# Inverses of 64x64 triangular blocks: 16x16 diagonal blocks by substitution on VectorE, and the old scan between its parts

## The chip, the cores and the metric

The kernel runs on one core of a Trainium2 chip. The metric is the time of one execution on the device in microseconds (us). TensorE is PE below, VectorE DVE, ScalarE ACT and GpSimd POOL.

## What is computed

A network in fp32 over 256 tokens of width 1024: two layers (feed-forward, three token mixers side by side, cross attention, feed-forward), and then one block with attention, a gated delta rule in both directions and a convolutional feed-forward. Two of the mixers are recurrences that are worked in chunks of 64 tokens, and each needs the inverse of a unit triangular 64x64 matrix per head and chunk. For the gated delta rule the reference says it so:

```python
kk = jnp.einsum('bhncd,bhnsd->bhncs', k, k)
a_mat = jnp.where(strict, beta[..., :, None] * dec * kk, 0.0) + jnp.eye(GDN_CHUNK, dtype=jnp.float32)
rhs = jnp.concatenate([beta[..., None] * v, (beta * jnp.exp(gam))[..., None] * k], axis=-1)
uw = lax.linalg.triangular_solve(a_mat, rhs, left_side=True, lower=True, unit_diagonal=True)
...
def step(s, inp):
    delta = u_c - jnp.einsum('bhcd,bhde->bhce', w_c, s)
    s_new = gl_c[..., None, None] * s + jnp.einsum('bhcd,bhce->bhde', kd_c, delta)
```

The layers' mixer (rwkv) is a recurrence per token in the reference; the kernel works it in chunks too, with an inverse of the same kind.

## The kernel before

`Inverse` inverts 16 tiles of 128x128, each with two 64x64 blocks on its diagonal, in 4 groups of 4 tiles, two groups (a pair) at a time with their instructions alternating. It goes by doubling: at level l (0 to 5) the inverses of blocks of size 2^l are joined to blocks of 2^(l+1). POOL makes the part of the matrix that belongs to the level (`inv_m` = `inv_d` x a mask), PE multiplies it by X, ACT copies the product to `inv_t`, PE multiplies that by the transposed inverse (`xt`) and by itself turned round, and DVE subtracts both results from X and `xt`. X and `xt` hold the inverse and its transpose. Level 0 is the identity minus the masked part (L1247). In the second block there is a seventh step, the join, which goes from 64 to 128.

The users are two. `rwkv_stage`, in each of two layers: 16 masked products `lt` on DVE (L1387), then the inverse, then `attention_stage`, which holds the layer's scan. And `gdn_stages`, with four quarters q (direction d = 0, 0, 1, 1, and half of the heads): per quarter four heads' matrices (`GdnMatrices`, the last product of each is L2717), then the inverse, then in the next quarter its scan (`GdnScan`, 12 steps). Steps 0 to 3 of the scan of q-1 lie between the matrices of q. Steps 4 to 11 are a chain in four rounds: PE multiplies by the state (L2779), DVE makes `gdelta` (L2817) and `gdk` (L2821), PE multiplies (L2786), DVE updates the state (L2830); in the last two rounds PE makes outputs (L2792, L2793), which ACT copies (L2851) for d = 0 and DVE adds (L2837) for d = 1. In the kernel before each of the steps 4 to 11 is issued ahead of one pair's level of the inverse of q, on PE, DVE and ACT alike:

```python
mats[q].inv.pe(pe, between=lambda pair: scan_step(pe, 4 + pair))
```

After quarter 3 the last scan is run alone ("quarter 4"). All engines execute in the order of their own queue and wait on semaphores. `K.dve_own.after` makes DVE wait for its own last instruction.

Of the kernel before, what the change touches and what calls it, by code (L numbers as in the profile page):

```python
# [35 lines left out]
LEVELS = 6  # L36
# [7 lines left out]
class Counted:  # L44


    def __init__(self, sem):
        self.sem = sem
        self.n = 0
# [23 lines left out]
def constant_tables():  # L73
# [23 lines left out]
    parts["blockident"] = brow == bcol  # L97
    for l in range(LEVELS):
# [3 lines left out]
    parts["levels_back"] = np.concatenate([m[1] for m in lev], 1)  # L102
    strict, incl = same & (row < col), same & (row <= col)
# [1070 lines left out]
class InversePlaces:  # L1174


    def __init__(self, K, ctx, groups, own_xt):
        f = lambda name: [K.sb(f"{name}{i}", [P, 4, CH], ctx=ctx) for i in range(2)]
        self.X, self.T1 = f("inv_x"), f("inv_t")
        self.diag = [K.sb(f"inv_d{g}", [P, 4, CH], ctx=ctx) for g in range(groups)]  # L1180
        self.xt = f("inv_xt") if own_xt else None
        self.mask = [[K.sb(f"inv_m{s}{j}", [P, 4, CH], ctx=ctx) for j in range(2)] for s in range(2)]


class Inverse:


    BLOCK_LEVELS = 6
    PER_GROUP = property(lambda self: self.BLOCK_LEVELS + (self.join is not None))

    def __init__(self, K, places, tag, groups, masks, lt, before, xt=None, join=None, bank=4):
        self.K, self.groups, self.masks = K, groups, masks
        self.lt, self.before, self.join = lt, before, join
# [4 lines left out]
        self.X, self.T1, self.diag, self.mask = places.X, places.T1, places.diag, places.mask  # L1198
        self.xt = xt or (lambda g: places.xt[g % 2][:, :, :])
# [4 lines left out]
        self.steps = [(pair * 2 + s, l) for pair in range(groups // 2) for l in range(self.PER_GROUP) for s in range(2)]  # L1204
        self.index = {st: i for i, st in enumerate(self.steps)}
        self.update = {st: i for i, st in enumerate([st for st in self.steps if st[1] > 0])}
        self.masked = {st: i for i, st in enumerate([st for st in self.steps if st[1] < self.BLOCK_LEVELS])}

    def finished(self, eng):

        eng.wait_ge(self.uv_ready, len(self.update))
        eng.wait_ge(self.t_copied, len(self.steps))
        eng.wait_ge(self.x_ready, len(self.update))
        if self.join is not None:
            eng.wait_ge(self.kept, 2 * self.groups)

    def final(self, g):

        return self.update[(g, self.PER_GROUP - 1)] + 1

    PAIRS = property(lambda self: len(self.steps) // 2)
    HALVES = (slice(0, CH), slice(CH, P))
# [5 lines left out]
    def pool(self, pool):  # L1228
        K = self.K
        for g, l in self.masked:  # L1230
            s = g % 2
            m = self.mask[s][l % 2]
            if l == 0:
                pool.wait_ge(self.d_ready, 2 * g + 2)
            if l >= 2:
                pool.wait_ge(self.t_ready, self.index[(g, l - 2)] + 1)
            elif g >= 2:
                pool.wait_ge(self.t_ready, self.index[(g - 2, self.BLOCK_LEVELS - 2 + l)] + 1)
            level = K.c(self.masks, first=l * CH, n=CH).unsqueeze(1).to_broadcast([P, 4, CH])
            ins = pool.tensor_tensor(m[:, :, :], self.diag[g][:, :, :], level, ALU.mult)  # L1240
            if l == 0:
                K.pool_own.after(pool, ins)
                if self.join is not None and g >= 2:
                    pool.wait_ge(self.x_ready, self.final(g - 2))
                    pool.wait_ge(self.kept, 2 * (g - 2) + 2)
                ident = K.c("blockident").unsqueeze(1).to_broadcast([P, 4, CH])
                ins = pool.tensor_tensor(self.xt(g), ident, m[:, :, :], ALU.subtract)  # L1247
            ins.then_inc(self.m_ready, 1)

    def blocks(self, pe, bank, lhsT, rhs):  # L1250

        for q in range(4):
            for half in self.HALVES:
                last = pe.matmul(bank[half, q * CH:(q + 1) * CH], lhsT[half, q, :], rhs(half, q), start=True, stop=True)  # L1254
        return last

    def pe(self, pe, between=lambda pair: None):

        K = self.K
        for i0 in range(0, len(self.steps), 2):  # L1260
            between(i0 // 2)
            for i in (i0, i0 + 1):
# [3 lines left out]
                X = lambda half, q: self.X[s][half, q, :]  # L1266
                if l == 0:
                    pe.wait_ge(self.m_ready, self.masked[(g, 0)] + 1)
                    last = self.blocks(pe, bank, self.xt(g), lambda half, q: K.c("blockident", half))
                elif l < self.BLOCK_LEVELS:  # L1270
                    pe.wait_ge(self.m_ready, self.masked[(g, l)] + 1)
                    if l == 1:
                        pe.wait_ge(self.t_copied, self.index[(g, 0)] + 1)
                    else:
                        pe.wait_ge(self.x_ready, self.update[(g, l - 1)] + 1)
                    last = self.blocks(pe, bank, self.mask[s][l % 2], X)
                else:
                    src, dst = self.joined()
                    pe.wait_ge(self.x_ready, self.update[(g, l - 1)] + 1)
                    for q in range(4):  # L1280
                        last = pe.matmul(bank[dst, q * CH:(q + 1) * CH], self.lt(g)[src, q, dst], X(src, q),
                                         start=True, stop=True)
                last.then_inc(self.t_ready, 1)
            if self.steps[i0][1] == 0:
                continue
            for i in (i0, i0 + 1):
# [3 lines left out]
                if l == 1 and g >= 2:  # L1290
                    pe.wait_ge(self.x_ready, self.final(g - 2))
                xt = lambda half, q: self.xt(g)[half, q, :]
                if l < self.BLOCK_LEVELS:
                    if l < self.PER_GROUP - 1:
                        self.blocks(pe, self.first_bank(s), self.xt(g), lambda half, q: self.T1[s][half, q, :])
                    last = self.blocks(pe, self.second_bank(s), self.T1[s], xt)
                else:
                    src, dst = self.joined()
                    for q in range(4):
                        last = pe.matmul(self.second_bank(s)[src, q * CH:(q + 1) * CH], self.T1[s][dst, q, :],  # L1300
                                         xt(dst, q), start=True, stop=True)
# [12 lines left out]
    def act(self, act, between=lambda pair: None, first=0):  # L1314
        for g in range(first, 2):
            self.diagonal(act, g)
        for i, (g, l) in enumerate(self.steps):
# [3 lines left out]
            if l == 2 and g + 2 < self.groups:  # L1321
                self.diagonal(act, g + 2)
            act.wait_ge(self.t_ready, i + 1)
            dst = self.X[s] if l == 0 else self.T1[s]
            rows = slice(0, P) if l < self.BLOCK_LEVELS else self.joined()[1]
            act.copy(dst[rows, :, :], self.psum(self.first_bank(s), rows)).then_inc(self.t_copied, 1)  # L1326
            if l == self.BLOCK_LEVELS:
                act.wait_ge(self.x_ready, self.update[(g, l - 1)] + 1)
# [3 lines left out]
    def dve(self, dve, between=lambda pair: None):  # L1332
        for i, (g, l) in enumerate(self.steps):
            if i % 2 == 0:
                between(i // 2)
            if l == 0:
                continue
            s = g % 2
            dve.wait_ge(self.uv_ready, self.update[(g, l)] + 1)
            if l < self.BLOCK_LEVELS:  # L1340
# [1907 lines left out]
```

## Time and profile before

| | us |
|---|---|
| median of 3 runs | 2956.34 (2944.53 to 2960.41) |
| the profiled execution | 2961.04 |
| its span | 2959.2 |
| PE busy | 2557.3 |
| DVE busy | 1139.4 |
| ACT busy | 1144.0 |
| POOL busy | 1303.1 |

The span is what the profile covers of the profiled execution. The granted clock is TensorE's as a share of its full 2.4 GHz (0.50 is 1.2 GHz); its mean over the execution is 0.912. In rows of the timeline the columns are start, duration, engine, line, operation, output<-inputs, shapes, count, and in brackets the engine's idle time ahead of it with what ended that.

### The profile page before, as it was taken

What the parts mean: (1) busy time and instruction counts of PE and PEld (TensorE: products, weight loads), DVE (VectorE), ACT (ScalarE), POOL (GpSimd) and SP (SyncE); (2) the same over time, 40 slices, a digit from 0 to 9 for tenths busy, and PEclk for the clock granted to TensorE, in tenths of its full rate; (3) what the DMA queues carried; (4) which work ended last, traced back from release to release, by engine and by line L of the source; (5) the groups of instructions that cost most, each with busy time, mean ns of one, the idle gap of its engine ahead of it and who ended that gap; (6) DMA issues with size and microseconds to landing.
All of it is one profiled execution on the core that took longest, in us unless ns stands there. A gap on an engine that the chain in (4) does not pass through costs nothing. (4 is left out here: it accounts for less than half of the span.)

```text
span 2959.2 us, 50697 instructions
## 1 busy us (share of the span) xinstructions
PE 2557.3 (86%) x22003; PEld 2228.7 (75%) x22003; DVE 1139.4 (39%) x2055; ACT 1144.0 (39%) x1567; POOL 1303.1 (44%) x452
## 2 busy tenths in 40 slices
PE   5998988886998998988977899699889997787878
PEld 4997865385997998966466899567667776787878
DVE  2113654332111111754242211276636664334990
ACT  4433422334443433422334442447833331533333
POOL 2774520151775774610043586322222121674655
PEclk8999988987999999988986999899979998898998
DMA  4554401431554554500432354422000000553432
GB/s 148 181 172 132 129 2 43 142 125 47 170 167 137 170 173 122 171 15 16 128 114 86 114 185 129 130 72 68 19 2 2 2 2 3 184 169 110 144 127 93
DMA packets 298722, 306.64 MB, mean 104 GB/s; under 512 B 7249, under 2 KB 294461, under 8 KB 298493
## 3 DMA queue, kind: packets, MB, share of 16 engines
q1 hardware_dynamic: 298493, 303.32, 31.9%
q8 instruction: 176, 2.88, 0.4%
q14 instruction: 53, 0.43, 0.0%
HBM read 302.25 MB, written 1.05 MB: 102 GB/s over the span
## 5 line engine op out<-in xcount | busy, mean ns | idle before, releaser
L360 POOL TENSOR_TENSOR slab_lo<-ring,slab_hi 128x2048 fp32r<-128x2048 f32 (+1 forms) x242 | 1096.2, 4539 | 1044.4 <-ACT slab_hi L351 1044.3
L351 ACT CAST slab_hi<-ring 128x2048 fp32r<-128x2048 f32 (+1 forms) x242 | 450.8, 1867 | 639.4 <-PE bank L383 579.2
L381 PE MATMUL bank<-ffn_h_hi,slab_hi 128*128 128x256 f32 x1408 | 402.5, 286 | 23.1 <-DVE ffn_h_lo L423 23.1
L382 PE MATMUL bank<-ffn_h_lo,slab_hi 128*128 128x256 f32 x1408 | 401.7, 285 | 0.0
L383 PE MATMUL bank<-ffn_h_hi,slab_lo 128*128 128x256 f32 x1408 | 401.5, 285 | 0.0
L381 PEld LDWEIGHTS bank<-ffn_h_hi,slab_hi 128*128 128x128 f32 x1408 | 273.8, 194 | 26.3 <-issue 26.3
L382 PEld LDWEIGHTS bank<-ffn_h_lo,slab_hi 128*128 128x128 f32 x1408 | 273.9, 195 | 0.0
L383 PEld LDWEIGHTS bank<-ffn_h_hi,slab_lo 128*128 128x128 f32 x1408 | 273.7, 194 | 0.0
L1240 POOL TENSOR_TENSOR inv_m<-inv_d,const 128x256 f32<-128x256 f32 x144 | 102.3, 725 | 347.9 <-ACT inv_d L1312 252.4
L590 DVE TENSOR_TENSOR hidden<-gate,bank 128x512 f32<-128x512 f32 x44 | 30.3, 688 | 456.6 <-PE bank L383 456.6
L381 PE MATMUL bank<-ffn_hidden_hi,slab_hi 128*128 128x256 f32 x704 | 199.6, 284 | 4.1 <-DVE hidden L590 4.1
L382 PE MATMUL bank<-ffn_hidden_lo,slab_hi 128*128 128x256 f32 x704 | 199.2, 283 | 0.0
L383 PE MATMUL bank<-ffn_hidden_hi,slab_lo 128*128 128x256 f32 x704 | 199.2, 283 | 0.0
L2192 POOL TENSOR_TENSOR tile_lo<-ring,tile_hi 128x1024 fp32r<-128x1024 f32 (+1 forms) x38 | 87.6, 2310 | 189.1 <-ACT tile_hi L2185 189.1
L381 PEld LDWEIGHTS bank<-ffn_hidden_hi,slab_hi 128*128 128x128 f32 x704 | 135.1, 192 | 4.9 <-DVE hidden L590 4.9
L382 PEld LDWEIGHTS bank<-ffn_hidden_lo,slab_hi 128*128 128x128 f32 x704 | 135.1, 192 | 0.0
L383 PEld LDWEIGHTS bank<-ffn_hidden_hi,slab_lo 128*128 128x128 f32 x704 | 135.1, 192 | 0.0
L381 PE MATMUL bank<-fh_hi,slab_hi 128*128 128x256 f32 x352 | 104.0, 296 | 35.5 <-POOL slab_lo L360 20.0
L3149 DVE SCALAR_TENSOR_TENSOR fcon<-fraw,prm,fcon 128x256 f32<-128x256 f32 x88 | 126.4, 1496 | 0.8
L2203 PE MATMUL bank<-both_hi,tile_hi 128*128 128x512 f32 (+2 forms) x296 | 107.8, 379 | 21.3 <-ACT tile_hi L2185 21.3
L1326 ACT COPY inv_t<-bank 128x256 f32<-128x256 f32 (+1 forms) x136 | 50.5, 371 | 165.3 <-PE bank L1254 142.6
L1599 PE MATMUL bank<-ring,cs 128*2 128x256 f32 x384 | 102.8, 394 | 0.0
(560 smaller groups left out, 6157.1 us busy)
## 6 DMA issues: line engine op xcount, KB each, us to landing
ring<-in_ffn_w_in SPq DMA_DIRECT2D x88, 1024.0 KB, 5.1
ring<-in_ffn_w_out SPq DMA_DIRECT2D x32, 1024.0 KB, 5.1
ring<-in_w_in SPq DMA_DIRECT2D x30, 1024.0 KB, 5.3
ring<-in_mix_w_in SPq DMA_DIRECT2D x24, 1024.0 KB, 5.4
ring<-in_w_mod SPq DMA_DIRECT2D x24, 1024.0 KB, 5.2
ring<-in_w_up SPq DMA_DIRECT2D x22, 1024.0 KB, 5.1
ring<-in_ffn_w_out SPq DMA_DIRECT2D x16, 768.0 KB, 4.4
ring<-in_mix_w_out SPq DMA_DIRECT2D x8, 1024.0 KB, 5.3
```

The costliest lines, as they stand in the source:

```text
L351: act.copy(self.hi[i % self.PLACES][:, 0:w], K.ring[n % RING][:, 0:w]).then_inc(self.hi_ready, 1)
L360: pool.tensor_tensor(self.lo[i % self.PLACES][:, 0:w], place[:, 0:w], self.hi[i % self.PLACES][:, 0:w].bitcast(F32), ALU.subtract).then_in ...
L381: pe.matmul(out, w[0], act[0], start=start, stop=False)
L382: pe.matmul(out, w[0], act[1], start=False, stop=False)
L383: return pe.matmul(out, w[1], act[0], start=False, stop=stop)
L590: dve.tensor_tensor(whole_hidden[:, i % 2, :], gate[:, i % 2, :], K.bank[2 * (i % 2) + 1][:, :], ALU.mult).then_inc(product_ready, 1)
L1240: ins = pool.tensor_tensor(m[:, :, :], self.diag[g][:, :, :], level, ALU.mult)
L1326: act.copy(dst[rows, :, :], self.psum(self.first_bank(s), rows)).then_inc(self.t_copied, 1)
L1599: last = pe.matmul(K.bank[self.BANKS[self.n % 2]][0:2, 0:HALF], K.cs[:, self.k, :], self.w[:, self.k, :], start=(self.k == 0), stop=(self. ...
L2192: last = pool.tensor_tensor(self.lo[u % self.PLACES][:, :, dst], self.source(u)[:, :, src], self.hi[u % self.PLACES][:, :, dst].bitcast(F3 ...
L2203: pe.matmul(out, hi[:, k, 0:m], both.hi[:, k, 0:tokens], start=(k == 0), stop=False)
L3149: last = dve.scalar_tensor_tensor(o[:, q, :], r[:, q, j:j + T], tap, o[:, q, :], ALU.mult, ALU.add)
```

## The change

Levels 0 to 3 go. The 16x16 diagonal blocks of all 16 tiles are inverted at once by substitution on DVE (`BlockSolve`), one 16x16 block in each partition: four transposes of 32x32 blocks bring them there (`dve_in`), six columns of two small operations invert the 8x8 halves (`dve_column`), two broadcast products with two reductions join the halves to 16x16 (`dve_join`), ACT and POOL spread the result with zeros (`widen`), and two transposes bring it back into X and `xt` (`dve_out`), which now hold all four groups. Then levels 4 and 5, and in the second block the join, are done as before, but with one order of waits (each step of the list waits for the update two steps before). The copies of the diagonals are made for all groups ahead of the levels.

In `gdn_stages` the steps 4 to 11 of the old scan are issued ahead of the whole inverse on PE and ACT, and on DVE between the parts of the substitution: `dve_in`, step 4, column 1, step 5, column 2, and so on to column 6, step 10, `dve_join`, step 11, `dve_out`, levels. Semaphores `mix_x_updated` and `xat_x_updated`, which are only counted up, are left out, and the constants hold masks for two levels in place of six, and the new masks.

```diff
-LEVELS = 6
+LEVELS = (4, 5)
...
+        self.turned, self.coef, self.solved = f("sol_turned", [P, 16, 32]), f("sol_coef", [P, 272]), f("sol_solved", [P, 272])
+        self.prod, self.part = self.turned[:, :, :].rearrange("p c r -> p (c r)"), f("sol_part", [P, 8, 8])
+        self.wide = [f(f"sol_wide{i}", [P, 16, 2, 32]) for i in range(2)]
...
+    def dve_in(self, dve):
+        K, p = self.K, self.p
+        for g, rows in enumerate(self.GROUPS):
+            src = self.lt[rows, :, 32 * g:32 * g + 32].rearrange("p u (b c) -> p c b u", b=2)
+            last = dve.transpose(p.turned[rows, :, :], src)
+        K.dve_own.after(dve, last)
+        coef = self.square(p.coef, swap=not self.upper)
+        K.dve_own.after(dve, dve.tensor_scalar(coef, p.turned[:, :, 0:16], K.c("halfrow", n=1), None, ALU.mult))
+        K.dve_own.after(dve, dve.scalar_tensor_tensor(coef, p.turned[:, :, 16:32], K.c("halfrow", first=1, n=1), coef,
+                                                      ALU.mult, ALU.add))
+        K.dve_own.after(dve, dve.tensor_tensor(p.solved[:, 0:256], p.coef[:, 0:256], K.c("strict16"), ALU.mult))
+        K.dve_own.after(dve, dve.memset(p.solved[:, 0:256:17], 1.0))
+
+    def dve_column(self, dve, j):
+
+        K, n = self.K, 7 - j
+        v, w = self.eighths(self.p.solved), self.eighths(self.p.coef)
+        prod = self.p.prod[:, 0:2 * n * j].rearrange("p (b c r) -> p b c r", b=2, c=n)
+        K.dve_own.after(dve, dve.tensor_tensor(prod, v[:, :, j:j + 1, 0:j].to_broadcast([P, 2, n, j]),
+                                               w[:, :, j + 1:8, j:j + 1].to_broadcast([P, 2, n, j]), ALU.mult))
+        K.dve_own.after(dve, dve.tensor_tensor(v[:, :, j + 1:8, 0:j], v[:, :, j + 1:8, 0:j], prod, ALU.subtract))
+
+    def dve_join(self, dve):
+        K, p = self.K, self.p
+        v = self.square(p.solved)
+        off = v[:, 8:16, 0:8]
+        prod = p.prod.rearrange("p (r j k) -> p r j k", r=8, j=8)
+        wide = [P, 8, 8, 8]
+        K.dve_own.after(dve, dve.tensor_tensor(prod, v[:, 0:8, 0:8].rearrange("p k r -> p r k").unsqueeze(2).to_broadcast(wide),
+                                               off.unsqueeze(1).to_broadcast(wide), ALU.mult))
+        K.dve_own.after(dve, dve.tensor_reduce(p.part[:, :, :], prod, mybir.AxisListType.X, ALU.add))
+        K.dve_own.after(dve, dve.tensor_tensor(prod, p.part[:, :, :].unsqueeze(2).to_broadcast(wide),
+                                               v[:, 8:16, 8:16].unsqueeze(1).to_broadcast(wide), ALU.mult))
+        dve.tensor_reduce(off.rearrange("p c r -> p r c"), prod, mybir.AxisListType.X, ALU.add).then_inc(self.solved, 1)
+
+    def dve_out(self, dve):
+        dve.wait_ge(self.widened, 8)
+        for i, dst in enumerate(self.targets):
+            dve.transpose(dst[:, :, :].rearrange("p u (b c) -> p c b u", b=4),
+                          self.p.wide[i][:, :, :, :].rearrange("p c a r -> p (c a) r")).then_inc(self.x_ready, 1)
+
+    def widen(self, eng, i, scaled):
+
+        eng.wait_ge(self.solved, 1)
+        src = self.square(self.p.solved, swap=(i == 0) == self.upper)
+        for a in range(2):
+            for b in range(2):
+                scaled(self.p.wide[i][:, :, a, 16 * b:16 * b + 16], src, self.K.c("quarterrow", first=2 * a + b, n=1))\
+                    .then_inc(self.widened, 1)
+
+    def act(self, act):
+        self.widen(act, 0, lambda out, src, scale: act.activation(out, src, ACT.Copy, scale=scale))
+
+    def pool(self, pool):
+        self.widen(pool, 1, lambda out, src, scale: pool.tensor_scalar(out, src, scale, None, ALU.mult))
...
     def act(self, act, between=lambda pair: None, first=0):
-        for g in range(first, 2):
+        for g in range(first, 4):
             self.diagonal(act, g)
+        self.solve.act(act)
...
+                    dve.wait_ge(intra_read, 16)
+                    inv.solve.dve(dve)
                     inv.dve(dve)
...
                     pe.wait_ge(mats[q].mats_read, GdnMatrices.HEADS)
-                    mats[q].inv.pe(pe, between=lambda pair: scan_step(pe, 4 + pair))
+                    for step in range(4, GdnScan.STEPS):
+                        scan_step(pe, step)
+                    mats[q].inv.pe(pe)
...
-                    mats[q].inv.dve(dve, between=lambda pair: scan_step(dve, 4 + pair))
+                    solve = mats[q].inv.solve
+                    dve.wait_ge(mats[q].mats_read, GdnMatrices.HEADS)
+                    solve.dve_in(dve)
+                    scan_step(dve, 4)
+                    for j in range(1, 7):
+                        solve.dve_column(dve, j)
+                        scan_step(dve, 4 + j)
+                    solve.dve_join(dve)
+                    scan_step(dve, 11)
+                    solve.dve_out(dve)
+                    mats[q].inv.dve(dve)
...
-                    mats[q].inv.act(act, first=2, between=lambda pair: scan_step(act, 4 + pair))
+                    for step in range(4, GdnScan.STEPS):
+                        scan_step(act, step)
+                    mats[q].inv.act(act, first=2)
```

## Rows read from the trace of the kernel before

**Rows 1.** The page, busy time of the engines.

```profile
PE 2557.3 (86%) x22003; PEld 2228.7 (75%) x22003; DVE 1139.4 (39%) x2055; ACT 1144.0 (39%) x1567; POOL 1303.1 (44%) x452
```

**Rows 2.** Timeline of the first layer, DVE where the inverse begins and ends.

```profile
406.31 1.29 DVE L1387 TENSOR_TENSOR lt<-bank,const 128x512 f32<-128x512 f32 x2 [1.56 <-PE bank L1378]
...
442.79 0.42 DVE L1343 TENSOR_TENSOR xt<-xt,bank 128x256 f32<-128x256 f32 x1 [0.27 <-PE bank L1254]
```

**Rows 3.** Windows of the second block: stretch, length, busy times, PEclk, DMA share, GB/s.

```profile
2180.60:2229.00 48.40, 42.41 (x1088) 39.79 (x1088) 17.83 (x49) 15.05 (x40) 15.65 (x22) 0.89 0.01 3
...
2255.70:2311.20 55.50, 50.47 (x1176) 46.32 (x1176) 30.04 (x81) 16.21 (x42) 17.82 (x26) 1.00 0.01 3
...
2484.40:2512.70 28.30, 17.02 (x88) 15.08 (x88) 10.90 (x34) 0.00 (x0) 0.00 (x0) 0.70 0.00 1
...
2489.00:2503.00 14.00, 8.25 (x33) 7.37 (x34) 5.35 (x18) 0.00 (x0) 0.00 (x0) 0.50 0.00 1
...
2204.00:2208.00 4.00, 3.20 (x66) 3.06 (x64) 0.00 (x0) 1.12 (x3) 3.92 (x7) 0.55 0.00 0
```

**Rows 4.** Timeline of a layer's and of quarter 0's doublings.

```profile
419.01 0.68 PE L1254 MATMUL bank<-inv_x,inv_m 64*64 64x64 f32 x16
...
425.09 1.10 PE L1254 MATMUL bank<-const,xt 64*64 64x64 f32 x32
425.30 0.42 DVE L1343 TENSOR_TENSOR xt<-xt,bank 128x256 f32<-128x256 f32 x1 [0.26 <-PE bank L1254]
...
2206.04 1.92 PE L1254 MATMUL bank<-inv_x,inv_m 64*64 64x64 f32 x32
...
2211.16 0.68 PE L1254 MATMUL bank<-inv_x,inv_m 64*64 64x64 f32 x16
...
2214.87 0.68 PE L1254 MATMUL bank<-inv_x,inv_m 64*64 64x64 f32 x16
...
2218.36 0.68 PE L1254 MATMUL bank<-inv_x,inv_m 64*64 64x64 f32 x16
...
2227.49 0.68 PE L1300 MATMUL bank<-inv_xt,inv_t 64*64 64x64 f32 x8 [0.36 <-ACT inv_t L1326]
...
2228.57 0.42 DVE L1348 TENSOR_SCALAR ring<-bank 64x256 f32<-64x256 f32 x1
```

**Rows 5.** Groups by form, DVE and POOL: busy us, mean ns of one.

```profile
L1387 DVE TENSOR_TENSOR lt<-bank,const 128x512 f32<-128x512 f32 x32 | 20.7, 688 | 27.2 <-PE bank L1378 27.2
...
L1342 DVE TENSOR_TENSOR inv_x<-inv_x,bank 128x256 f32<-128x256 f32 x112 | 47.2, 421 | 113.8 <-PE bank L1254 113.5
...
L1152 DVE TENSOR_TENSOR es<-cum 128x12 f32<-128x12 f32 x2 | 0.4, 180 | 0.1
...
L1240 POOL TENSOR_TENSOR inv_m<-inv_d,const 128x256 f32<-128x256 f32 x144 | 102.3, 725 | 347.9 <-ACT inv_d L1312 252.4 <-PE bank L1254 95.1
...
L2192 POOL TENSOR_TENSOR tile_lo<-ring,tile_hi 128x128 fp32r<-128x128 f32 x2 | 0.9, 464 | 0.0
```

**Rows 6.** Timeline of quarter 4's scan, and two groups of ACT.

```profile
2485.61 0.69 DVE L2817 TENSOR_TENSOR gdelta<-ring,bank 128x512 f32<-128x512 f32 x1 [3.93 <-PE bank L2779]
...
2487.26 1.68 PE L2786 MATMUL bank<-gdk,g_ktok 128*128 128x128 f32 x8 [1.69 <-DVE gdk L2821]
...
2493.92 2.08 PE L2786 MATMUL bank<-gdk,g_ktok 128*128 128x128 f32 x8 [1.69 <-DVE gdk L2821]
...
2507.01 1.16 PE L2779 MATMUL bank<-gstate,gxt 128*128 128x128 f32 x8 [1.28 <-DVE gstate L2830]
...
2508.93 0.88 DVE L2821 TENSOR_SCALAR gdk<-gdelta,g_kdec 128x128 f32<-128x128 f32 x4
...
2511.95 0.69 DVE L2837 TENSOR_TENSOR go<-go,bank 128x512 f32<-128x512 f32 x1 [2.15 <-PE bank L2793]
...
L2851 ACT COPY go<-bank 128x512 f32<-128x512 f32 x4 | 2.3, 585 | 12.9 <-PE bank L2793 12.9
...
L1312 ACT COPY inv_d<-ring 64x256 f32<-64x256 f32 x32 | 12.9, 403 | 0.6
```

More of the change, by code:

```diff
@@ L102, in constant_tables @@
     parts["levels_back"] = np.concatenate([m[1] for m in lev], 1)
+    half, quarter = i % 32 // 16, i // 32 % 2
+    parts["halfrow"] = np.stack([half == b for b in range(2)], 1)
+    parts["quarterrow"] = np.stack([(quarter == a) & (half == b) for a in range(2) for b in range(2)], 1)
+    parts["strict16"] = np.tile(-np.tril(np.ones((16, 16)), -1).reshape(1, 256), (P, 1))
     strict, incl = same & (row < col), same & (row <= col)
@@ L1196, in __init__ @@
+class Inverse:
+    JOIN = 6
+    HALVES = (slice(0, CH), slice(CH, P))
+    def __init__(self, K, places, tag, masks, lt, before, xt=None, join=None, bank=4):
+        self.K, self.groups, self.masks = K, 4, masks
+        self.before, self.join = before, join
+        self.lt = lambda g: lt[:, 4 * g:4 * g + 4, :]
         self.first_bank = lambda s: K.bank[bank + 2 * s]
         self.second_bank = lambda s: K.bank[bank + 1 + 2 * s]
-        self.X, self.T1, self.diag, self.mask = places.X, places.T1, places.diag, places.mask
@@ L1228, in pool @@
     def pool(self, pool):
[L1229 to L1248, printed above, removed]
+        for pair in range(2):
+            for l in LEVELS:
+                for s in range(2):
+                    g = 2 * pair + s
+                    pool.wait_ge(self.d_ready, 2 * g + 2)
+                    if pair:
+                        pool.wait_ge(self.t_ready, self.index[(s, l)] + 1)
+                    level = self.K.c(self.masks, first=(l - LEVELS[0]) * CH, n=CH).unsqueeze(1).to_broadcast([P, 4, CH])
+                    pool.tensor_tensor(self.mask[s][l % 2][:, :, :], self.diag[g][:, :, :], level, ALU.mult)\
+                        .then_inc(self.m_ready, 1)
+            if pair == 0:
+                self.solve.pool(pool)
     def blocks(self, pe, bank, lhsT, rhs):
@@ L1289, in pe @@
                 pe.wait_ge(self.t_copied, i + 1)
[L1290 to L1296, printed above, removed]
+                if l != self.JOIN:
+                    if l != self.last:
+                        self.blocks(pe, self.first_bank(s), self.xt(g), self.T1[s])
+                    last = self.blocks(pe, self.second_bank(s), self.T1[s], self.xt(g))
                 else:
@@ L1320, in act @@
                 between(i // 2)
-            if l == 2 and g + 2 < self.groups:
-                self.diagonal(act, g + 2)
             act.wait_ge(self.t_ready, i + 1)
[L1324 to L1328, printed above, removed]
+            rows = slice(0, P) if l != self.JOIN else self.joined()[1]
+            act.copy(self.T1[s][rows, :, :], self.psum(self.first_bank(s), rows)).then_inc(self.t_copied, 1)
+            if l == self.JOIN:
+                act.wait_ge(self.x_ready, 2 + self.index[(g, l - 1)] + 1)
                 for half in self.HALVES:
@@ L1879, in mix_out_stage @@
     n0 = K.eaten
-    x_updated = K.sem("mix_x_updated")
     with ExitStack() as ctx:
```

112 lines of the change are left out of this document (58 added, 54 removed).

## The prediction, made before the changed kernel had run

> **What bounds the kernel now.** I read the page first for the engines' shares [rows 1]: TensorE is busy for 86% of the 2959.2 us span, but that is an average, and the change touches none of the stages that make it. So I looked for the stretches that hold the inverses: one in each of the two layers, one in each of four quarters of the second block. In the timeline the layer's stretch begins where DVE has written the last `lt` (406.31 + 1.29 = 407.60) and ends with the last `xt` update (442.79 + 0.42 = 443.21): 35.6 us [rows 2]; the second layer repeats it. In the second block I cut the windows from the last masked product (L2717) to the last join (L1348): 48.4 us for quarter 0, which has no old scan beside it, 55.5 for quarter 1, and quarters 2 and 3 repeat that within 0.2 [rows 3]. What comes next waits for the inverse, so what is won or lost in such a stretch is won or lost in the span. Inside, one level of doubling for a pair of groups takes 3.49 us (2214.87 to 2218.36) [rows 4], a ring of PE, ACT, PE and DVE in which each waits for the one before. No DMA and no slab work is issued there, so no transfer moves.
>
> The decisive comparison: with nothing beside it, the old scan takes 28.3 us for its eight steps (quarter 4) [rows 3]; between the doublings it adds only 55.5 - 48.4 = 7.1 us, because it fills their waits, and the clock reads 1.00. The change takes that cover away and puts the substitution there instead.
>
> **The doublings that stay.** In a layer they are levels 4 and 5 for two pairs. From the first product of level 4 (419.01) to the next pair's first product (425.09) it is 6.1 us, and to the last update (425.30 + 0.42) 6.7: 12.8 for both. In a quarter, levels 4, 5 and the join take from 2218.36 to 2228.57 + 0.42, 10.6 us, and to the end of the last join product (2227.49 + 0.68) 9.8: 20.4 for both pairs [rows 4]. PE comes to them after a long idle. Where the granted clock had fallen, to 0.55 [rows 3], a level took from 2206.04 to 2211.16, 5.1 us for 3.5 [rows 4]. I add that 1.6 once: 14.4 in a layer, 22.0 in a quarter.
>
> **The substitution.** No row shows a DVE transpose or a reduction, or ScalarE or POOL scaling by a column, so I price them by element. DVE's 128x512 in 0.688 and 128x256 in 0.421 us give 0.155 us + 1.04 ns per element. The one row whose operands step far at every element (L1152, 12 elements 64 words apart) takes 0.180: 12.5 ns more, so 2.1 ns per element [rows 5]. A wait for the engine's own last operation I take as 0.03. A transpose here steps far on one side and is contiguous on the other: I take 1.6 ns, midway, and keep 1.04 and 2.1 as ends.
> Coming in: four transposes of 512 elements, 0.155 + 0.82 = 0.97 each, less 0.2 of overlap, 3.7; four operations of 256 elements or fewer (0.35, 0.42, 0.42, 0.07) with waits, 1.4. Together **5.1**.
> Six columns: twelve operations of at most 24 elements, 0.20 + 0.03 each: **2.8**.
> Join of the eighths: one product with a far step 0.97, a contiguous product and two reductions 0.69 each, waits 0.1: **3.1**.
> Widening: four operations on ACT and four on POOL side by side. POOL's two-input 128x256 takes 0.725 and its 128x128 0.464 [rows 5]; with one input I take 0.6, so **2.5** with the semaphore; ends 2.0 and 3.0. ACT's copies of a half are 0.40 [rows 6], with a column as scale I take 0.45, so 1.8.
> Going out: PE starts after the first transpose of 1024 elements, 0.155 + 1.64 = **1.8**; the second lies beside PE's first products and ACT's copy.
> From the last mask to PE's first product: 15.3 us; ends 12.6 and 17.9.
>
> The Trainium skill, page "Vector Engine (DVE) Microarchitecture Reference", section "Measured stream behaviour on trn2", speaks against the low end: a port keeps its rate only over runs of two or more adjacent words; a hop at every element costs about 1.7 ns on one side, small steps on the sources 2.5. No row here has such a stream of length. By it, as an estimate, each solve costs 0.8 us more than my 15.3, and the whole 5 us more.
>
> **Layers:** 15.3 + 14.4 = 29.7 against 35.6: -5.9 each, **-11.8**. The masks on POOL and the diagonals on ACT lie beside DVE's work. **Quarter 0:** 15.3 + 22.0 = 37.3 against 48.4: **-11.1**.
>
> **Quarters 1 to 3.** PE now issues all eight scan steps before its first doubling, so the inverse is queued behind the whole scan on PE, DVE and ACT. First the scan's first delta waits on DVE for the 5.1 of coming in. Then comes the chain that quarter 4 shows alone: from the first delta (2485.61) to the end of the last dk (2508.93 + 0.88) 24.2 us. PE's products ran at 0.50 of the clock there [rows 3], 2.08 us for a group that takes 1.16 at full clock; the first took 1.68 and will be cold too after a longer wait: 24.6. The columns cost nothing: each (0.46) lies in DVE's wait of over 2.08 for PE; with that cover gone they would add 2.8 a quarter. After the last dk ACT is the late one in quarters 1 and 2: output products 2.1 (2509.81 to 2511.95), copy of `go` 0.58, the diagonals of groups 2 and 3, now queued behind the scan's steps, 1.6 [rows 6], widening 1.8: 6.1, where join and POOL need 5.6. Then 1.8 and 22.0. Together 5.1 + 24.6 + 6.1 + 1.8 + 22.0 = 59.6 against 55.5: +4.1 each. In quarter 3 DVE adds the scan's output and ACT is early, so join and POOL decide, 5.7 with the added operation's edge: 59.2, +3.7. Together **+11.9**.
> The Trainium skill, page "GPSIMD Engine Reference", section "Performance pitfalls for Q7 kernels", says that reads with a step over 8 bytes cost 2.9 instead of 1.9 cycles per element. POOL reads the turned square in quarters 2 and 3; by it, as an estimate, its four widenings take 0.9 us longer there. No row shows such a read.
>
> The removed semaphores, for which nobody waits, and the narrower constants are 0. Sum: -11.8 - 11.1 + 11.9 = **-11.0 us**. The profiled execution took 2961.04 (1.8 around its span), 4.7 above the median of 2956.34; the same saving from the median gives about **2945**.
>
> **The rivals.**
> B, the streams run at full rate (1.04 ns everywhere, POOL at 0.464, ACT at 0.40). Solve 12.6: layers -17.2, quarter 0 -13.8, the others +2.0, +2.0, +1.0: -26.0, 2930. For it: DVE's masked product reads a broadcast pattern without loss. Against it: L1152. Chance 0.18.
> C, every far step costs 2.1, and POOL takes 0.725. Solve 17.9: layers -6.6, quarter 0 -8.5, others +18.3: +3.2, 2959.5. Chance 0.09.
> D, PE keeps its full clock through the scan: five groups at 1.16 for 2.08, 4.6 a quarter, -24.8 in all, 2931.5. Against it: 14 us of quarter 4 at 0.50; for it: today's stretches of quarters 1 to 3 are all at 1.00 [rows 3]. Chance 0.10.
> E, the other side: 32x32 blocks of four-byte elements go through DVE's transpose slower than any stream assumed. On the path are 4 x 512 + 1024 = 3072 elements, six times. It decides for slower from (14.8 + 11.0)/6 = 4.3 us a solve, 1.4 ns more per element, so from 3.0 ns on. At 4.2, twice the far step, it is 8.0 us a solve, +37 in all, 2993. For it: no transposing operation is in the trace, and L1152 shows that one element a cycle isn't given. Against: nothing shows a rate of 3 ns on DVE for so simple an operation. Chance 0.13.
> The forecast, 0.50, with a range of its own from 2936 to 2957.
>
> **The numbers.** Within 0.5%, about what a measurement here can tell, is 14.8 us either way. Faster: B, D and the low part of the forecast (0.12), 0.40. Slower: E and a remainder of C, 0.14. Same: 0.46. The range from 2928 to 2975 takes in B, C, D and the near part of E.
>
> **What would show it.** In the profile after: each layer's stretch about 30 us, quarter 0's about 37; quarters 1 to 3 about 59.5, with a granted clock near 0.5 in the middle and product groups of 2.08; transposes of 1.0 and 1.8 us; columns inside DVE's waits for PE; ACT's widening ending after POOL's in quarters 1 and 2. The prediction is wrong if the transposes leave 1 to 2.1 ns per element, if the clock holds through the scan, or if a column or the widening is longer than its cover.

## The result, and the profile after

The changed kernel takes 2961.68 us (median; 2958.39 to 2966.62) beside 2956.15 for the kernel before on the same chips: a ratio of 1.0025, 95% interval 1.0014 to 1.0036: slower, by some 7 us by the ratio and by 5.5 us between the medians. The prediction was 2945, 11 us faster. The granted clock, averaged over the profiled execution, is 0.885 for 0.912.

The page after, the line that answers to [rows 1]:

```profile
PE 2449.8 (83%) x18163; PEld 2128.3 (72%) x18163; DVE 1162.5 (39%) x2067; ACT 1121.9 (38%) x1495; POOL 1241.7 (42%) x356
```

TensorE lost 107.5 us of busy time (2557.3 - 2449.8) and the kernel is no shorter. The stretches of [rows 2, 3] have to be read again.

First the timeline of the first layer after, DVE with ACT and POOL at the widening and PE's first product (start, duration, engine, line):

```profile
403.62 1.29 DVE L1454 TENSOR_TENSOR lt<-bank,const 128x512 f32<-128x512 f32 x2 [1.56 <-PE bank L1445]
404.95 4.16 DVE L1219 STREAM_TRANSPOSE sol_turned<-lt 32x512 f32<-32x512 f32 x4
...
410.55 0.07 DVE L1226 MEMSET sol_solved<- 128x16 f32 x1
410.66 0.18 DVE L1233 TENSOR_TENSOR sol_turned<-sol_solved,sol_coef 128x12 f32<-128x12 f32 x1
...
411.51 0.18 DVE L1233 TENSOR_TENSOR sol_turned<-sol_solved,sol_coef 128x24 f32<-128x24 f32 x1
...
413.23 1.02 DVE L1243 TENSOR_TENSOR sol_turned<-sol_solved 128x512 f32<-128x512 f32 x1
...
415.72 0.69 DVE L1248 TENSOR_REDUCE sol_solved<-sol_turned 128x64 f32<-128x512 f32 x1
420.16 1.93 DVE L1253 STREAM_TRANSPOSE inv_x<-sol_wide 128x1024 f32<-128x1024 f32 x1 [3.75 <-POOL sol_wide L1269]
...
422.15 1.97 PE L1335 MATMUL bank<-inv_x,inv_m 64*64 64x64 f32 x32 [17.96 <-DVE inv_x L1253]
...
435.77 0.42 DVE L1410 TENSOR_TENSOR xt<-xt,bank 128x256 f32<-128x256 f32 x1 [0.27 <-PE bank L1335]
...
416.45 2.57 ACT L1266 ACTIVATE sol_wide<-sol_solved,const 128x256 f32<-128x256 f32 x4 [10.67 <-DVE sol_solved L1248]
...
416.51 3.62 POOL L1269 TENSOR_SCALAR sol_wide<-sol_solved,const 128x256 f32<-128x256 f32 x4 [19.98 <-DVE sol_solved L1248]
```

From the end of the last `lt` (404.91) to the end of the last `xt` (436.19) it is 31.3 us, where before had 35.6. The transpose out waits 3.75 us, and the wait is put down to POOL's widening: ACT's four take 2.57 us, POOL's 3.62. The second layer is 31.1, before 35.5. Both together gain 8.7 us, 11.8 were forecast.

The windows of the second block after: quarter 0, quarter 1, and in quarter 1 the first two rounds of the old scan (stretch, length, busy times, granted clock, DMA share, GB/s):

```profile
2163.60:2202.30 38.70, 18.46 (x448) 17.22 (x448) 23.13 (x50) 10.85 (x26) 6.48 (x8) 0.72 0.01 2
...
2229.10:2293.50 64.40, 39.08 (x536) 35.66 (x536) 32.15 (x82) 12.82 (x30) 8.10 (x11) 0.68 0.00 1
...
2234.90:2249.00 14.10, 8.16 (x32) 7.12 (x32) 6.42 (x26) 0.00 (x0) 0.00 (x0) 0.50 0.00 0
```

Quarter 0 takes 38.7 us for 48.4 [rows 3], a gain of 9.6 before rounding (11.1 forecast). Quarter 1 takes 64.4 for 55.5 (the first product of its doublings stands at 2271.32, its last join ends at 2293.53); quarter 2 (2319.04 to 2383.65) 64.6 and quarter 3 (2407.50 to 2472.42) 64.9, each for 55.7: losses of 9.0, 8.9 and 9.2, where 4.1, 4.1 and 3.7 were forecast. -8.7 - 9.6 + 27.0 = +8.7 us: within the interval of the measured ratio (4 to 11 us). The two profiled spans differ by 0.5 us only, because stages that the change does not touch were some 8 us shorter in this one execution; the runs together don't show that.

Where quarter 1 lost it, in the timeline around the last dk of the old scan and from there on, all engines:

```profile
2257.71 1.16 PE L2846 MATMUL bank<-gstate,ring 128*128 128x128 f32 x8 [1.31 <-DVE gstate L2897]
...
2259.69 0.87 DVE L2888 TENSOR_SCALAR gdk<-gdelta,g_kdec 128x128 f32<-128x128 f32 x4
2260.48 1.02 DVE L1243 TENSOR_TENSOR sol_turned<-sol_solved 128x512 f32<-128x512 f32 x1
...
2260.62 0.79 PE L2859 MATMUL bank<-gqdec,gstate 128*128 128x128 f32 x2 [1.75 <-DVE gdk L2888]
...
2262.97 0.69 DVE L1248 TENSOR_REDUCE sol_solved<-sol_turned 128x64 f32<-128x512 f32 x1
...
2263.76 0.63 PE L2860 MATMUL bank<-gpt,gdelta 128*128 128x128 f32 x2
...
2264.43 0.58 ACT L2918 COPY go<-bank 128x512 f32<-128x512 f32 x1 [7.42 <-PE bank L2860]
2265.04 1.69 ACT L1383 COPY inv_d<-ring 64x256 f32<-64x256 f32 x4
2266.76 2.56 ACT L1266 ACTIVATE sol_wide<-sol_solved,const 128x256 f32<-128x256 f32 x4
2269.34 1.92 DVE L1253 STREAM_TRANSPOSE inv_x<-sol_wide 128x1024 f32<-128x1024 f32 x1 [5.68 <-ACT sol_wide L1266]
```

The product group at 2257.71 is the state's product of the last round. Read the rest from the bottom: the transpose out waits for ACT, whose widening stands behind the diagonals, behind the copy of `go`, behind TensorE's output products (2260.62 to 2264.39). It is 8.8 us from the last dk's end, where 6.1 were forecast. In quarter 2 the same transpose waits for POOL instead, whose four widenings are longer there:

```profile
2353.30 4.48 POOL L1269 TENSOR_SCALAR sol_wide<-sol_solved,const 128x256 f32<-128x256 f32 x4 [32.66 <-DVE sol_solved L1248]
2354.55 1.70 ACT L1266 ACTIVATE sol_wide<-sol_solved,const 128x256 f32<-128x256 f32 x4
2357.81 1.92 DVE L1253 STREAM_TRANSPOSE inv_x<-sol_wide 128x1024 f32<-128x1024 f32 x1 [4.61 <-POOL sol_wide L1269]
```

### The profile page after: what moved, and what is told of

It reads as the page before. It is cut to its first block and busy times, and to the rows that moved or that the text cites. A ratio compares the mean times of both kernels' runs of the same rounds, so it can differ in the third digit from the quotient of the medians.

```text
span 2959.7 us, 42799 instructions
## 1 busy us (share of the span) xinstructions
PE 2449.8 (83%) x18163; PEld 2128.3 (72%) x18163; DVE 1162.5 (39%) x2067; ACT 1121.9 (38%) x1495; POOL 1241.7 (42%) x356
## 5 line engine op out<-in xcount | busy, mean ns | idle before, releaser
L1326 POOL TENSOR_TENSOR inv_m<-inv_d,const 128x256 f32<-128x256 f32 x48 | 34.3, 725 | 308.4 <-ACT inv_d L1383 266.1
L1335 PE MATMUL bank<-inv_x,inv_m 64*64 64x64 f32 x768 | 37.4, 252 | 81.5 <-DVE inv_x L1253 58.1
L385 PE MATMUL bank<-fh_lo,slab_hi 128*128 128x256 f32 x352 | 104.1, 296 | 0.0
```

Of the source, the lines that this page charges most:

```text
L385: pe.matmul(out, w[0], act[1], start=False, stop=False)
L1326: pool.tensor_tensor(self.mask[s][l % 2][:, :, :], self.diag[g][:, :, :], level, ALU.mult)\
```

## The experiments

No kernel leaves work out. Times are medians of several runs, each with the ratio to the kernel before on the same chip (2957 to 2960 us there) and its 95% interval.

**Either block alone.** The first run puts the new inverse into the two layers only, the old one stays in the second block:

> The new inverse in the two layers alone; the second block inverts and scans as in the kernel before. Theory S (the loss is the old scan, which now stands at half clock between the substitution's parts instead of between the doublings; the substitution itself gains): the layers' stretches are 31.2 us for 35.6 and the rest is unchanged, so 8.7 us less than the kernel before, ratio 0.997. Rival L (what the layers gain in their stretch is given back in the attention stage that follows, by a colder TensorE): ratio 1.000. Rival W (the substitution is a loss in itself): over 1.000.

2943.8 us, 0.9952 [0.9931, 0.9972]; its first layer stretch is 31.0 us (410.03 to 441.05). The gain there is real and reaches the end of the kernel; the forecast of 0.997 lies just inside the interval. The other half has the new inverse in the second block only (to make it fit, `sol_part` lies in `inv_t0`):

> The change in the second block alone; the two layers keep the doublings of before. It is the other half of the run with the change in the layers alone (ratio 0.9952). The stretches of the trace of after say: quarter 0 shorter by 9.65 us, quarters 1 to 3 longer by 9.0, 8.9 and 9.4, 17.6 in all for the second block, and the layers give 8.8 of it back. So this kernel takes 17.6 us more than before, ratio 1.006, and its quarters are those of after. Rival: part of the loss came from the layers' new code or from the longer stages around, and this kernel is at the 1.0025 of the whole change.

2972.8 us, 1.0052 [1.0027, 1.0077]. Its quarters repeat those of after: 38.7 for quarter 0, 64.6 for quarter 2. The two halves (-0.0048 and +0.0052) put together give +0.0004 with an interval of some 0.003 either way, which takes in the 1.0025. The loss is in quarters 1 to 3.

**Where the old scan's steps stand.** Two steps stay in the substitution, six go back between the six pairs of doublings:

```diff
-                    for step in range(4, GdnScan.STEPS):
-                        scan_step(pe, step)
-                    mats[q].inv.pe(pe)
+                    for step in range(4, 6):
+                        scan_step(pe, step)
+                    mats[q].inv.pe(pe, between=lambda pair: scan_step(pe, 6 + pair))
```

(ACT and DVE alike; on DVE step 4 behind `dve_in`, step 5 behind the columns.)

> As the changed kernel, but only steps 4 and 5 of the old scan lie in the substitution (after the blocks are brought in, and after the columns), and steps 6 to 11 lie ahead of the six pairs of doublings on TensorE, DVE and ACT. Theory S: in quarters 1 to 3 the stretch is 5.8 + 1.6 + 2.6 + 1.1 + 3.2 + 3.7 + 1.9 = 20 us to TensorE's first product of the inverse, then 22 and some 6.5 for six steps between the doublings, 48.5 in place of 64.5 us: 48 us less than the changed kernel in all, about 2914. Rival W (the substitution and not the scan's place makes these quarters long): at least 60 us a quarter, 2950 or more.

2925.7 us, 0.989 [0.9866, 0.9914]. With four steps in the substitution and four among the doublings:

> As two_four, but steps 4 to 7 of the old scan lie in the substitution and steps 8 to 11 ahead of the first four pairs of doublings. Theory S: 23.3 us to the inverse's first product, then 22 and 5 for four steps with the output products: 50.5 us a quarter in place of 64.5, 42 us less than the changed kernel, about 2920, and 6 us slower than two_four. Rival W: 2950 or more.

2932.2 us, 0.9915 [0.9892, 0.9937]. The difference of 6.5 us between the two medians is near the 6 expected, though their intervals overlap; both stand 12 us above their expectations. Quarters 1 and 2 of the first are 51.5 and 52.2 us where I had reckoned 48.5: POOL's widening (3.75 us) was still in the sum as forecast, and TensorE's product of step 6 (2.08 us) turned out to stand in front of the first doubling. The other way, with all eight steps ahead of the substitution on DVE:

```diff
-                    solve.dve_in(dve)
-                    scan_step(dve, 4)
-                    for j in range(1, 7):
-                        solve.dve_column(dve, j)
-                        scan_step(dve, 4 + j)
-                    solve.dve_join(dve)
-                    scan_step(dve, 11)
+                    for step in range(4, GdnScan.STEPS):
+                        scan_step(dve, step)
+                    solve.dve_in(dve)
+                    for j in range(1, 7):
+                        solve.dve_column(dve, j)
+                    solve.dve_join(dve)
```

> The kernel after the change, with the eight steps of the old scan on VectorE ahead of the whole substitution, none between its parts. Theory: VectorE's parts of the substitution (5.8 us in, 2.6 of columns, 3.2 of join) lie in waits of the scan in after and come onto the path here: a quarter is 2 to 4 us longer than in after, rounds are 7.0 us, 2968 to 2974. Rival: the steps between the parts delay the substitution and the scan as much as they hide, and the time stays at 2961.

2969.9 us, 1.0048 [1.0029, 1.0066], 8 us above after. The intervals of these two overlap, but the trace shows where the time went: the quarters are 64.8, 67.0 and 68.7 us, 6.5 longer together than in after. So the times line up: eight steps ahead 2970, among the parts of the substitution 2962, half of them among the doublings 2932, six of them 2926. The windows of the run with two and six, quarters 1 (its last join ends at 2283.51, 1.1 us before the window does) and 2:

```profile
2232.00:2284.60 52.60, 34.07 (x537) 30.94 (x538) 34.01 (x88) 12.30 (x29) 8.17 (x11) 0.76 0.01 1
2310.30:2362.60 52.30, 32.66 (x536) 29.93 (x536) 33.45 (x83) 11.57 (x29) 9.05 (x11) 0.77 0.01 1
```

Quarter 2 takes 52.2 us (2310.35 to 2362.57): 12.4 less than after, with the same operations. Two chains of waits lie in a quarter: that of the doublings and that of the scan. Where they stand one behind the other, each is paid.

**What the half clock costs.** In quarter 1 of after a round of the scan (delta to delta) takes 7.2 us. The first attempt to raise the clock has products of constants into an unused bank behind the steps, fourteen behind steps 4 and 11 and three behind each of the others:

```diff
                     for step in range(4, GdnScan.STEPS):
                         scan_step(pe, step)
+                        if q:
+                            keep_busy(K, pe, K.bank[7], 14 if step in (4, 11) else 3)
```

> The changed kernel with products of constants into a bank that nobody reads, 3 behind each scan step on TensorE in quarters 1 to 3 and 14 behind steps 4 and 11, so that TensorE does not idle; nothing else differs and the output is the same. Theory S with the clock as its main term: the granted clock in the scan is near 1.00 for 0.57, the chain from the first delta to the last dk takes about 19.5 us for 25.7, the outputs and the first level of doubling 3 us less: 8 to 9 us a quarter, 25 us in all, about 2937. Rival Q (the queueing alone costs it, not the clock): the quarters stay at 64 us or grow by the added products, 2961 or more.

2977.2 us, 1.0066 [1.0041, 1.009]: 40 us beside the expectation. TensorE's timeline in this run:

```profile
2231.59 8.32 PE L433 MATMUL bank<-const 128*128 128x512 f32 x19
2239.74 1.05 PE L2853 MATMUL bank<-gdk,g_ktok 128*128 128x128 f32 x8
2240.63 2.74 PE L433 MATMUL bank<-const 128*128 128x512 f32 x6
```

Three constant products are six records and 2.74 us. They outlast the wait that they were put into, and the scan's own products queue behind them: TensorE has no idle time there, the clock is 1.00, and the rounds are 11.9, 6.9 and 8.7 us. The fourteen behind step 11 then hold up the first doubling: the transpose out begins 42.6 us into quarter 1 and TensorE's first product 49.6, in after 40.3 and 42.3. The run tested the filler, not the clock. With five, eight and one in place of fourteen, fourteen and three:

> The kernel after the change, with products of constants into an unused bank in quarters 1 to 3: five behind step 4, eight behind step 11, and one behind each step between. In the run with three and fourteen the granted clock was 1.00 in the whole scan, but each constant product took 0.87 us, not the 0.43 that was reckoned, and three of them (2.7 us) outlasted the wait of 1.5 us they were put into: rounds took 7.0 us again, and the first 11.8. With one (0.87 us) the products fit into the wait. If the half clock is what made the rounds 7.2 us, they go to 5.4, the output products behind step 11 take 1.9 us in place of 3.8, and a quarter is some 8 us shorter: about 2937. If the clock does not stay full with so little, rounds stay at 7.1 and the time at 2961. If the rounds were 7.2 us for VectorE's columns and waits, the clock is full and the rounds stay at 7.

2937.5 us, 0.9937 [0.9912, 0.9961], 24 us below after. The window of three rounds of quarter 1, and DVE's timeline at the ends of the first two:

```profile
2235.90:2253.70 17.80, 13.10 (x75) 8.93 (x76) 9.61 (x39) 0.59 (x1) 0.00 (x0) 1.00 0.00 1
```

```profile
2235.86 0.69 DVE L2884 TENSOR_TENSOR gdelta<-ring,bank 128x512 f32<-128x512 f32 x1
...
2241.21 0.69 DVE L2884 TENSOR_TENSOR gdelta<-ring,bank 128x512 f32<-128x512 f32 x1 [1.01 <-PE bank L2846]
...
2246.57 0.69 DVE L2884 TENSOR_TENSOR gdelta<-ring,bank 128x512 f32<-128x512 f32 x1 [1.01 <-PE bank L2846]
```

The first two rounds take 5.35 us at a clock of 1.00 for 7.2 at 0.50, with DVE's columns unchanged between them. The transpose out of quarter 1 begins 32.4 us into the quarter (2262.42 - 2230.04), in after 40.3. The quarters take 55.0, 56.1 and 57.5 us, 9.4, 8.5 and 7.5 less than in after: 25.4 of the 27.0 that the change lost there. At full clock, then, the new inverse behind the scan costs about what the old one cost with the scan inside (55.5 to 55.7 us). The order with two and six takes 51.5, 52.2 and 51.8 us without any filler, so laying one chain into the other gains more than the full clock alone does; how that gain divides between the cover and the clock (0.76 and 0.77 there, 0.68 and 0.71 in quarters 1 and 2 of after) no run here separates.

**The widening.** POOL's four go to DVE, in front of `dve_out`:

> The kernel after the change, with GpSimd's four widenings of each inverse given to VectorE (behind the old scan's last step, ahead of the two transposes out). In the trace of after, GpSimd's four take 3.62 us in a layer and in quarters 0 and 1 and 4.48 in quarters 2 and 3, ScalarE's four 2.56 and 1.70. If the widenings are at the path's end where GpSimd is the later engine, the transposes out begin about 1.1 us sooner in both layers and in quarter 0, 1.5 in quarter 2, 2.0 in quarter 3, and no sooner in quarter 1, where ScalarE ends last behind its copy of the outputs: 6.8 us in all, 2955. Rival: VectorE's own widenings with a column's scale and a strided source take as long as GpSimd's, and then there is no gain, or a loss of up to 4 us per quarter.

2952.3 us, 0.9991 [0.9974, 1.0008]. The group of the new operations:

```profile
L1251 DVE TENSOR_SCALAR sol_wide<-sol_solved,const 128x256 f32<-128x256 f32 x24 | 7.5, 376 | 0.2
```

376 ns for what takes POOL 993. The median is 9 us below after's, and the interval ends below that of after (1.0008 against 1.0014), narrowly: the gain is there, its size uncertain. In quarter 1 the transposes began 2.4 us sooner where none was expected; there the output products of step 11, and the second half of step 9's, ran at 0.39 instead of 0.63 us a pair, so the clock did that, not the widening. Then ACT's order as well, the diagonals ahead of step 4 and the widening ahead of step 11:

```diff
+                    for g in range(2, 4):
+                        mats[q].inv.diagonal(act, g)
-                    for step in range(4, GdnScan.STEPS):
+                    for step in range(4, GdnScan.STEPS - 1):
                         scan_step(act, step)
-                    mats[q].inv.act(act, first=2)
+                    mats[q].inv.solve.act(act)
+                    scan_step(act, GdnScan.STEPS - 1)
+                    mats[q].inv.act(act, first=4)
```

> The kernel with VectorE's widenings (2952.3, its trace: transposes out 37.9, 37.4 and 37.6 us into quarters 1, 2 and 3), and on ScalarE the copies of the diagonal blocks of groups 2 and 3 ahead of the old scan's step 4 and the widenings ahead of step 11, whose copy of the outputs they stood behind. In that trace VectorE waits 2.76 us for ScalarE's last widening in quarter 1. If ScalarE's order is what is late there, the transposes out start 2.9 us sooner in quarter 1 (2.6 us of widening behind the join's end, in place of copy, diagonals and widening), about 1.3 sooner in quarter 2, and no sooner in quarter 3, whose scan has no such copy: 4 us, 2948. Rival: what is saved there is waited for again behind step 11's products, and the time stays at 2952.

2953.1 us, 0.9989 [0.997, 1.0008]: nothing that the runs can tell. In the trace the order does what it says:

```profile
2262.11 2.57 ACT L1267 ACTIVATE sol_wide<-sol_solved,const 128x256 f32<-128x256 f32 x4 [6.69 <-DVE sol_solved L1248]
2264.58 0.57 ACT L2915 COPY go<-bank 128x512 f32<-128x512 f32 x1
```

The transposes out start 36.6, 36.6 and 37.5 us into quarters 1 to 3, for 37.9, 37.4 and 37.6 without it: 2.1 us in all, below the scatter of the runs. The 4 us that I expected were too many in quarter 1, since DVE still waits for ACT behind its own 1.14 us of widening:

```profile
2264.71 1.94 DVE L1254 STREAM_TRANSPOSE inv_x<-sol_wide 128x1024 f32<-128x1024 f32 x1 [1.46 <-ACT sol_wide L1267]
```

**A version that beats both.** Two steps in the substitution, six among the doublings, widenings on DVE:

> Two steps in the substitution and six among the doublings (2925.7 before), with the widenings of GpSimd on VectorE. If widenings and scan are priced apart, the gain is that of the run with VectorE's widenings alone, about 1.1 us in each layer and in quarter 0, and now also in quarter 1 (where ScalarE has no output copy ahead of it) and some 2 in quarters 2 and 3: about 8 us, 2918. Rival: no change, 2925.

2913.6 us, 0.9863 [0.9837, 0.9889]. It beats the kernel before and after; that DVE's widenings help here too, the runs alone do not show (the interval overlaps with that of 0.989 above), but the quarters do, 48.7, 48.8 and 50.0 us. Then with TensorE's product of step 6 ahead of its wait for the inverse:

> Two steps in the substitution and six among the doublings, widenings on VectorE (2913.6), with TensorE's product of step 6 ahead of its wait for the inverse. In the trace of the run without it, that product (2.08 us at half clock) starts when the first transpose out has ended, ahead of the first doubling's products, once in each of quarters 1 to 3. Moved up it lies beside the join: 2.0 us less per quarter, 6 in all, 2907.6. Rival: TensorE has then been idle for longer when the doublings begin, their first products run at half clock for longer, and half of it is given back.

2909.5 us, 0.9845 [0.9818, 0.9873]. From the last `ring` of quarter 1 to the last delta of the last scan it is 229.5 us, 232.8 without: 3.3 gained of the 6 expected; the interval overlaps with the one before, so the gain rests on these two traces. (The profiled execution took 2928.6 us, 19 above the median, 18 of them ahead of quarter 0.) Last, the same with constant products in the substitution and in the last quarter's scan:

> The kernel of the run with the early product, and products of constants into an unused bank: five behind step 4, two behind step 5, seven behind step 6 in quarters 1 to 3, and one behind each of steps 4 to 10 of the last quarter's scan. Clock theory: granted clock 1.00 in the substitution of quarters 1 to 3, step 5's product 0.9 us shorter and the first doublings at full clock, 2 to 3 us per quarter; in the last quarter two rounds at 5.2 in place of 7.1 us and output products at full clock, 5 us: 11 to 14 us less than without them, about 2895. Rival: the constant products stand in the way of the real ones, as three behind each step did, and nothing is gained.

2908.8 us, 0.9841 [0.9814, 0.9869]: no gain for the 11 to 14 us expected. The filler worked where it stood (the last scan's four deltas span 17.5 us, 21.9 without). Most of it was lost elsewhere. Windows of quarter 1's first doublings, its last scan steps and the preparation of quarter 2, in the run with filler:

```profile
2256.00:2263.70 7.70, 7.51 (x178) 7.00 (x179) 5.62 (x19) 0.76 (x3) 2.11 (x4) 1.00 0.02 4
...
2273.60:2284.00 10.40, 8.92 (x147) 7.65 (x147) 5.82 (x20) 3.58 (x9) 0.00 (x0) 0.90 0.01 2
2284.00:2309.20 25.20, 24.14 (x127) 17.86 (x125) 17.91 (x59) 10.04 (x22) 1.22 (x2) 0.84 0.00 1
```

and the same without filler:

```profile
2265.70:2274.30 8.60, 8.59 (x188) 8.07 (x185) 6.13 (x19) 1.13 (x4) 2.62 (x4) 0.87 0.01 4
...
2284.30:2294.30 10.00, 8.52 (x147) 7.33 (x146) 5.46 (x19) 3.58 (x9) 0.00 (x0) 1.00 0.01 2
2294.30:2316.90 22.60, 21.55 (x127) 16.50 (x125) 18.04 (x61) 10.03 (x22) 1.21 (x2) 0.92 0.01 1
```

The first doublings are 0.9 us shorter with filler, the next parts 0.4 and 2.6 longer, at a lower clock (0.90 and 0.84 for 1.00 and 0.92). What the filler won early was gone before quarter 2. Whether the one causes the other is not shown: these are two executions, and the clock of a stretch with the same code differs between executions too (quarter 2 of the run with the layers alone, whose second block is that of before, took 57.0 us at 0.97 for 55.7 at 1.00).

## Why the prediction was wrong

The mechanism was forecast: gains in the layers and in quarter 0, losses in quarters 1 to 3, where the chain of the scan comes ahead of the doublings at half clock. The direction of the sum was not, since nearly every price was taken too low, and they add: 19.7 us over two layers and four quarters turned -11.0 into +8.7. The step that failed is the price of quarters 1 to 3, +11.9 forecast and +27.0 measured; in it, over the three quarters, "after the last dk" was 6.3 us too low, the doublings 3.9, coming in 2.6, the chain of the scan 2.2. That the measured 2961.68 still lies in the range from 2928 to 2975, and within the 0.5% that had a chance of 0.46, is the width of these two and no merit of the sum: it lies outside the forecast's own 2936 to 2957. By the prediction's own steps:

- **The gains, -11.8 and -11.1.** Measured -8.7 and -9.6. From the last mask to PE's first product a layer takes 17.2 us (404.91 to 422.15) for 15.3. That is 0.6 of coming in, 1.25 of widening, 0.1 of going out, less 0.2 of columns and with 0.1 of join. The 14.4 of doublings were 14.0.
- **"With one input I take 0.6", so 2.5 for POOL's widening: the step that failed in the layers and quarter 0.** It measured 0.905 each there (3.62 for four) and 3.75 with the semaphore, outside the stated ends of 2.0 and 3.0. An operation with one operand fewer was not the cheaper, 0.905 for the 0.725 of the nearest row. Whether the column as scale or the widened write makes it so, no run separates.
- **Coming in 5.1.** Measured 5.7 in a layer and up to 6.1 in quarters 2 and 3. The 32x512 transposes took 1.037 us each, those out 1.923. With 0.155 us + c per element, as in the prediction, these give c = 1.72 and 1.73 ns. I took 1.6, midway between 1.04 and 2.1. The 2.1 had no footing: it was read from L1152's 0.180 us for 12 elements, and after's columns take 0.18 for 12 and for 24 elements alike, so that the 12.5 ns are not the price of a step. The Trainium skill, page "Vector Engine (DVE) Microarchitecture Reference", section "Measured stream behaviour on trn2", gives about 1.7 ns per element for a stream that hops at every element on one side; it measured other operations than the transpose, and the trace agrees with it. Rival E, from 3.0 ns on, is refuted, though its sign came out; so are B and C. That C's 2959.5 us comes nearest to the measured time is luck: its 2.1 ns and its 0.725 are both wrong.
- **The chain of the scan, 24.6.** Measured 25.7, 25.0 and 25.3: right to 1.1 us. Each column did lie in DVE's wait for PE (rounds of 7.2 us beside 7.1 alone), and the run with all steps ahead shows what the cover of the whole substitution is worth: 8 us between the medians, 6.5 in the quarters. Rival D, a clock that stays full, is refuted by 0.50 in the window above.
- **"After the last dk", 6.1: the largest single error.** Measured 8.8, 7.7 and 7.7 us. In quarter 1 the output products take 3.8 us for the 2.1 that I read in quarter 4 [rows 6]: there the granted clock was 1.00 in them; here it had come back for the product group of 1.16 us at 2257.71 and was down to 0.50 again from 2260.6 to 2264.4. In quarter 2 it was 1.00 in them and they took 2.1. And ACT's widening took 2.56 for 1.8, its source being the turned square; in quarter 2, where it is not, the four took 1.70. In quarters 2 and 3 the square is turned for POOL instead, and POOL is the late one: four take 4.48 us, 1.12 each for 0.905. The Trainium skill's page "GPSIMD Engine Reference", section "Performance pitfalls for Q7 kernels", gives reads with a step over 8 bytes half as much again per element; the trace agrees with the 0.9 us for four that I had estimated by it (4.48 - 3.62), which is a quarter more for the whole operation. I had left this out of the sum.
- **22.0 of doublings.** Measured 22.2 in quarter 1 and 23.9 and 23.8 in quarters 2 and 3 (clock 0.81 in these for 0.88). With the filler, at a clock near 1.00, they are 20.6 to 20.8, beside the 20.4 that I had without a cold start: the 1.6 us for it was half of what it cost in quarters 2 and 3.
- **The place of the eight steps.** The prediction said rightly that "the inverse is queued behind the whole scan", priced it too low, and then let the shorter substitution pay for it. The runs show how large that price is: 36 us between all steps in the substitution and six of them among the doublings, more than the new inverse gains in the layers and quarter 0 together (18.3).

Open stays whether the clock or the cover gives most of those 36 us, how much of the 9 us of DVE's widening is the clock's chance, and why the filler's gain in the best version was given back.

## What to carry to other kernels

Two chains of waits on the same engines should cover each other. Before moving one out from under the other, add up both lengths: a shorter replacement of one (here 9.6 us less in quarter 0) does not make up for paying the other (25 us) in the open. Where a stretch turns sparse, price all its products at the lower clock: here the output products behind the last round took 3.8 us for the 2.1 read elsewhere, and the first doublings were slow too. A filler must be shorter than the wait it is put into, or it is the wait. And an operation that no row shows is worth a range that reaches above its nearest row: here nearly all errors had one sign, and the inverse stands in six places.

## What the runs showed of the hardware beyond that

- POOL against DVE for the same operation with a column as scale, 128x256, mean over strided and contiguous sources (after, and the run with DVE's widenings): 993 and 376 ns. ACT took 2.56 us for four where the source was strided and 1.70 where it was contiguous; POOL 4.48 and 3.62.
- A reduction of 128x512 to 128x64 costs DVE what the product of that size costs (685 and 692 ns); the product with the far step took 1022.
- A 128x128 by 128x512 product in fp32 is two records of the trace and some 0.9 us at full clock (2.74 for three). I had taken one record for the product and so made the first filler twice too long.
